# Decode lots of a paged attention in eight pieces of one matmul form each, values in one piece, no closing product

## The reference, cut to what matters

```
def fox_attend(q, c_q, segments):          # 8 heads of 64
    for k, _, c_k, mask in segments:
        s = einsum('bqhd,bkhd->bhqk', qf, k) + cq - c_k
    p = softmax(concatenate(logits, axis=-1))
    for k, v, _, _ in segments:            # past pages, then the new tokens
        out += einsum('bhqk,bkhd->bqhd', p[..., start:start + n], v)

def wkv_step(S, inp):                      # the recurrence, token by token
    sa = einsum('bhij,bhj->bhi', S, a_t)
    S = S * w_t + sa * b_t + v_t * k_t
    y = einsum('bhij,bhj->bhi', S, r_t)
```

## Time and profile before

| | us |
|---|---|
| median of 3 runs | 1510.46 |
| lowest, highest | 1509.58, 1511.0 |
| profiled execution, its time | 1510.73 |
| profiled execution, span from first to last instruction | 1509.0 |
| lots and recurrence steps, within the span | 331 to 912 |

### The profile page before, as it was taken

How to read it: one execution, slowest core, us unless ns; L and a number is a source line. 1 busy time by engine, 2 the same in 40 slices (tenths; PEclk the granted TensorE clock), 3 DMA queues, 4 the chain that set the end, 5 groups by cost and what they waited for, 6 DMA issues and landing times.

```text
span 1509.0 us, 27895 instructions
## 1 busy us (share of the span) xinstructions
PE 1402.4 (93%) x11595; PEld 953.3 (63%) x11595; DVE 438.2 (29%) x917; ACT 357.0 (24%) x713; POOL 110.0 (7%) x223
## 2 busy tenths in 40 slices
PE   5999999988799999999989779999999999999997
PEld 4755666655577777777755454477777777744442
DVE  5022355455844444444445241310000000000002
ACT  3010233245444343443433331100000000000011
POOL 6283000000000000001202010000000000000000
PEclk9999899998799999999989889999999999999998
DMA  5187011023898787878957897003111221150001
GB/s 206 57 189 205 7 57 35 1 75 110 284 312 277 229 292 247 294 255 266 272 191 261 315 314 245 1 13 100 56 56 56 89 79 56 56 195 0 0 0 63
DMA packets 123174, 219.32 MB, mean 145 GB/s; under 512 B 11451, under 2 KB 35078, under 8 KB 123046
## 3 DMA queue, kind: packets, MB, share of 16 engines
q1 hardware_dynamic: 115154, 193.64, 38.3%
q0 software_dynamic: 7824, 23.85, 5.9%
q10 hardware_dynamic: 68, 0.02, 0.0%
HBM read 203.06 MB, written 14.41 MB: 144 GB/s over the span
## 4 chain that ended last, share of the span: by engine, by line
PE 84%; DVE 5%; DMA 4%; ACT 3%; issue 2%; SPq 1%; POOL 0%; DVEq 0%; POOLq 0%; ACTq 0%
PE PS L1369 23%; PE PS L736 13%; PE PS L1388 10%; PE PS L1178 6%; PE PS L1192 4%; PE PS L1308 4%; PE PS L1237 4%; PE PS L709 2%; DMA arena<-in_cache_k 2%; DMA out_wkv_prompt<-arena 1%; PE PS L1394 1%; PE PS L992 1%; PE PS L1002 1%; PE PS L996 1%; ACT arena L1622 1%
## 5 line engine op out<-in xcount | busy, mean ns | idle before, releaser
L1369 PE MATMUL PS<-arena 128*128 128x288 f32 x1408 | 342.1, 405 | 1.2 <-DVE arena L2251 1.2
L1369 PEld LDWEIGHTS PS<-arena 128*128 128x128 f32 x1408 | 265.7, 189 | 77.4 <-DVE arena L2251 1.4
L736 PE MATMUL PS<-arena 128*128 128x301 f32 (+1 forms) x736 | 197.7, 426 | 0.0
L1622 ACT ACTIVATE arena<-PS 128x512 f32<-128x512 f32 x256 | 141.4, 596 | 192.8 <-PE PS L1178 192.4
L1178 PE MATMUL PS<-arena 128*128 128x128 f32 x1024 | 153.8, 296 | 27.1 <-DMA arena<-in_cache_k 15.1
L736 PEld LDWEIGHTS PS<-arena 128*128 128x128 f32 (+1 forms) x736 | 136.6, 189 | 54.7 <-issue 13.6
L1178 PEld LDWEIGHTS PS<-arena 128*128 128x128 f32 x1024 | 122.1, 151 | 55.8 <-issue 24.2
L1388 PE MATMUL PS<-arena 128*128 128x512 f32 x352 | 151.5, 592 | 1.5 <-DVE arena L2277 1.5
L1388 PEld LDWEIGHTS PS<-arena 128*128 128x128 f32 x352 | 66.5, 189 | 86.2 <-issue 84.3
L2277 DVE TENSOR_TENSOR arena<-PS,arena 128x576 f32<-128x576 f32 x22 | 16.7, 758 | 327.0 <-ACT arena L1686 327.0
L1686 ACT ACTIVATE arena<-PS 128x576 f32<-128x576 f32 x22 | 14.3, 651 | 329.8 <-PE PS L1369 329.8
(11 more groups left out here) (360 smaller groups left out, 1409.9 us busy)
## 6 DMA issues: line engine op xcount, KB each, us to landing
arena<-in_cache_k SPq DMA_DIRECT2D x256, 256.0 KB, 4.3
arena<-in_cache_v SPq DMA_DIRECT2D x256, 256.0 KB, 4.8
arena<-in_w_gate SPq DMA_DIRECT2D x11, 1024.0 KB
arena<-in_w_up SPq DMA_DIRECT2D x11, 1024.0 KB
arena<-in_w_in SPq DMA_DIRECT2D x5, 2048.0 KB, 11.9
forgets_after<-arena POOLq DMA_DIRECT2D x64, 128.0 KB, 8.5
arena<-forgets_after SPq DMA_DIRECT2D x32, 256.0 KB, 5.1
arena<-in_w_down SPq DMA_DIRECT2D x4, 2048.0 KB
```

The costliest lines, as they stand in the source:

```text
L736: ins = mm(PS[0:width, bank, 0:HALF], wring[:, c % 2, k, c0:c0 + width], xnT[:, k, half * HALF:(half + 1) * HALF], start=(k == 0), stop=(k ...
L1369: ins = mm(PS[:, 4 * (f % 2) + 2 * w + half, 0:HO], fring[r % FR][:, c:c + P], hT[:, k, half * HO:(half + 1) * HO], start=(k == 0), stop=( ...
L1622: av(KTs[:, (2 * i + q) % LOT], PS[:, T_USE[("k", L, i, q)] % 2, :].rearrange("p (g n) -> p g n", g=NG), ACT.Copy)\
```

## The change

- The pieces of lot L on TensorE are now: (0) keys 0; (1) scores 3 of lot L-1, and at a pair's first lot new_scores; (2) keys 1; (3) scores 0; (4) keys 2, then the turned probabilities of lot L-1; (5) scores 1; (6) keys 3, at a pair's first lot after turn_new; (7) scores 2 and all four value pages of lot L-1, at a pair's first lot also new_values, then turn_output. Scores 3 of the last lot come behind the loop.
- ScalarE: exp_lot(L-1) follows take_keys(L, 1) in piece 2 (before: it came ahead of it). VectorE: add_scores(L-1), and add_new, move to piece 1; take_probs to 4, add_sums to 5, add_output to 7.
- The closing product is gone; add_output waits for the count v_free of the last value product, and ov_ready now counts new_values alone.
- SyncE loads key pages 0 to 3 of a lot and then value pages 0 to 3 of the one before.
- A table RWKV_DUE gives one step after nearly every odd piece, and after an even one where the steps have fallen behind (20 or so in all). The last step comes after piece 239 of 256, before after 236.

```
--- before.py
+++ after.py
@@ -288,20 +288,25 @@
             T_READ.append((reader, n))
 
         for L in range(LOTS + 1):
-            for i in range(LOT + 1):
-                if i == 2 and L:
+            for i in range(LOT):
+                if i == 3 and L:
                     use_t(("p", L - 1), "pr_taken", L)
-                if i < LOT and L < LOTS:
+                if i == 3 and L % NLOT == 0 and L < LOTS:
+                    use_t(("n", L // NLOT), "prn_taken", L // NLOT + 1)
+                if L < LOTS:
                     for q in range(2):
                         use_t(("k", L, i, q), "kt_taken", 2 * LOT * L + 2 * i + q + 1)
-                if L % NLOT == 0:
-                    if i == 2 and L < LOTS:
-                        use_t(("n", L // NLOT), "prn_taken", L // NLOT + 1)
-                    if i == 3 and L:
-                        use_t(("o", L // NLOT - 1), "o_done", L // NLOT)
+            if L % NLOT == 0 and L:
+                use_t(("o", L // NLOT - 1), "o_done", L // NLOT)
+
+        RWKV_DUE = []
+        for piece in range(8 * LOTS):
+            done, aim = RWKV_DUE[-1] if piece else 0, 1 + (piece + 1) * N_RWKV / (8 * LOTS - 14)
+            RWKV_DUE.append(min(N_RWKV, done + (done < aim if piece % 2 else done < aim - 1)))
+        assert RWKV_DUE[-1] == N_RWKV
 
         def rwkv_due(piece):
-            return min(N_RWKV, 1 + piece * (N_RWKV - 1) // (8 * LOTS - 20))
+            return RWKV_DUE[piece]
 
         x2 = at(XR0, NTILE, D)
         hT = at(qT_off, KT, OUTC)
@@ -443,14 +448,10 @@
                 if not first:
                     load_bias(pr, j)
                 numbers = lot_numbers(pr, j)
-                for i in range(3):
+                for i in range(LOT):
                     key_page(pr, j, numbers, i)
                 if vj is not None:
-                    for i in range(2):
-                        value_page(vpr, vj, value_numbers, i)
-                key_page(pr, j, numbers, 3)
-                if vj is not None:
-                    for i in range(2, LOT):
+                    for i in range(LOT):
                         value_page(vpr, vj, value_numbers, i)
                 if first:
                     load_bias(pr, j)
@@ -1227,18 +1228,15 @@
                              start=True, stop=True, skip_group_check=True)
                 ins.then_inc(S["ov_ready"], 1)
 
-            def lot_values(L, half):
-                if half == 0:
-                    pe.wait_ge(S["pr_taken"], L + 1)
-                    pe.wait_ge(S["ov_taken"], L + L // NLOT + 1)
-                for i in range(2 * half, 2 * half + 2):
+            def lot_values(L):
+                pe.wait_ge(S["pr_taken"], L + 1)
+                pe.wait_ge(S["ov_taken"], L + L // NLOT + 1)
+                for i in range(LOT):
                     pe.wait_ge(v_in[i], 32 * (L + 1))
                     for r in range(4):
                         ins = mm(PS[ROWS[r], OUT, 0:QW], PTs[:, i, ROWS[r]], Vr[:, i, r // 2, QW * (r % 2):QW * (r % 2) + QW],
                                  start=(i == 0), stop=(i == LOT - 1), skip_group_check=True)
                     ins.then_inc(S["v_free"], 1)
-                if half:
-                    mm(PS[:, OUT, 511:512], ident, ones[:, 0:1], start=False, stop=True, skip_group_check=True).then_inc(S["ov_ready"], 1)
 
             def turn_output(pr):
                 pe.wait_ge(S["o_scaled"], pr + 1)
@@ -1252,33 +1250,32 @@
                     pr, j = L // NLOT, L % NLOT
                     turn_keys(L, 0)
                     yield
+                    if L:
+                        page_scores(L - 1, 3)
+                    if j == 0 and L:
+                        new_scores(pr)
+                    yield
                     turn_keys(L, 1)
+                    yield
                     page_scores(L, 0)
                     yield
+                    turn_keys(L, 2)
                     if L:
                         turn_probs(L - 1)
                     yield
-                    turn_keys(L, 2)
                     page_scores(L, 1)
                     yield
-                    if L:
-                        lot_values(L - 1, 0)
                     if j == 0:
                         turn_new(pr)
-                    yield
                     turn_keys(L, 3)
+                    yield
                     page_scores(L, 2)
-                    yield
                     if L:
-                        lot_values(L - 1, 1)
-                    yield
-                    page_scores(L, 3)
+                        lot_values(L - 1)
                     if j == 0:
+                        new_values(pr)
                         if L:
                             turn_output(pr - 1)
-                        new_values(pr)
-                    if j == NLOT - 1 and pr + 1 < NPAIR:
-                        new_scores(pr + 1)
                     yield
 
             pe.wait_ge(S["proj_taken"], len(ITEMS))
@@ -1292,6 +1289,8 @@
                     next(rest)
                     done += 1
             assert done == N_RWKV and next(rest, 1) == 1
+
+            page_scores(LOTS - 1, 3)
 
             def rows_of(i):
                 return (slice(64, P), slice(SEQ, OUTC)) if i == 0 else (slice(0, P), slice((i - 1) * P, i * P))
@@ -1320,8 +1319,7 @@
             project(0)
             turn_probs(LOTS - 1)
             project(1)
-            for half in range(2):
-                lot_values(LOTS - 1, half)
+            lot_values(LOTS - 1)
             project(2)
             turn_output(NPAIR - 1)
             project(3)
@@ -1636,18 +1634,18 @@
                     pr, j = L // NLOT, L % NLOT
                     take_keys(L, 0)
                     yield
+                    yield
+                    take_keys(L, 1)
                     if L:
                         exp_lot(L - 1)
-                    take_keys(L, 1)
+                    yield
                     yield
                     if L and j == 0:
                         exp_new(pr)
-                    yield
                     take_keys(L, 2)
                     yield
                     yield
                     take_keys(L, 3)
-                    yield
                     yield
                     yield
 
@@ -2136,12 +2134,12 @@
 
             def add_output(L):
                 q = L // NLOT % 2
-                dve.wait_ge(S["ov_ready"], L + L // NLOT + 2)
+                dve.wait_ge(S["v_free"], LOT * (L + 2))
                 dve.wait_ge(S["ov_taken"], L + L // NLOT + 1)
                 stt(Ov[:, q], Ov[:, q], Sb[:, L % 2, 0:1], PS[:, OUT, 0:QW], ALU.mult, ALU.add).then_inc(S["ov_taken"], 1)
 
             def first_output(pr):
-                dve.wait_ge(S["ov_ready"], (NLOT + 1) * pr + 1)
+                dve.wait_ge(S["ov_ready"], pr + 1)
                 v.tensor_copy(Ov[:, pr % 2], PS[:, OUT, 0:QW]).then_inc(S["ov_taken"], 1)
 
             def scale_output(pr):
@@ -2167,28 +2165,29 @@
                     pr, j = L // NLOT, L % NLOT
                     yield
                     if L:
-                        add_sums(L - 1)
+                        add_scores(L - 1)
+                    if j == 0 and L:
+                        add_new(pr)
+                    yield
+                    yield
                     yield
                     if L:
                         take_probs(L - 1)
                     yield
+                    if L:
+                        add_sums(L - 1)
                     yield
                     if j == 0:
                         take_new_probs(pr)
                     yield
-                    yield
                     if L:
                         add_output(L - 1)
-                    if j == 0 and L:
-                        scale_output(pr - 1)
-                    yield
-                    add_scores(L)
                     if j == 0:
                         if L:
+                            scale_output(pr - 1)
+                        first_output(pr)
+                        if L:
                             take_output(pr - 1)
-                        first_output(pr)
-                    if j == NLOT - 1 and pr + 1 < NPAIR:
-                        add_new(pr + 1)
                     yield
 
             dve.wait_ge(S["rn_taken"], 1)
@@ -2252,6 +2251,7 @@
                 ins.then_inc(S["xnT_ready"], 1)
 
 
+            add_scores(LOTS - 1)
             add_sums(LOTS - 1)
             take_probs(LOTS - 1)
             add_residual(0)
```

96 lines of the change are left out of this document (47 added, 49 removed).

## The result

The changed kernel takes 1539.79 us (median of 4 runs, 1530.01 to 1548.62), the kernel before 1510.47 beside it (1509.58 to 1511.0): ratio 1.0193, 95% interval 1.0131 to 1.0255. It is slower by 29 us, where the prediction had 6.5 less. The four runs of the changed kernel had mean TensorE clocks of 0.936, 0.941, 0.944 and 0.951 of full speed, with 1548.6, 1538.9, 1540.7 and 1530.0 us: by and large its time follows its clock. The profiled execution is the slowest of them (1548.6 us, span 1546.8).

What follows compares the result with a forecast made beforehand. TensorE's own stream was taken to bound 412 to 780 us, waits or bytes other stretches. Savings 13.3 + 13.5, less 11.7, 7.0 and 1.4, gave 6.7 us: 1504.0 us from 1510.73, range 1492 to 1514.

Steps and rivals of the forecast that it cites:

- the two crowded stretches: SyncE's loads around the output weights and the residual inputs: less slack but less queued behind, 0, ends 6 us either way.
- rival (e): Twelve transposes in a row take the clock to 1.2 GHz for one keys piece a lot: 27 us, 1531; chance 0.02.
- Recurrence steps: -1.4 us (ends 0 and -5): Steps whose answer is not fully covered by pieces: five more TensorE waits of 0.2 to 0.3 us each.
- Closing product, 9.6 + 0.3: Two instructions a lot removed: 0.31 us in each of 31 lots, and 0.3 us for the last lot's.
- Rival (d): Closing product nearly free, its 0.31 us going into what follows: 8 us less gain, 1512; chance 0.03.
- Probabilities behind keys 2: In piece 4 the turned probabilities wait for ScalarE's copy to free a PSUM bank: 26 lots x 0.45, -11.7 us.
- rival (a): The bank wait is the long one, ScalarE's step copies ahead each time: 7.3 us more, 1511; chance 0.15.
- The pair chain: At lots 8, 16 and 24, scores 0 wait for add_new, behind ScalarE's later exponential: 3 x 2.3, -7.0 us.
- a clock below 1.00 there: Sign in ordinary lots of the middle stretch, 412 to 780 us, that would make the prediction wrong.
- rival (b): Value burst in SyncE's queue between piece 7 and the next piece 1 starves loads: 22 us, 1526; chance 0.10.
- The sum for the middle: Lots 4 to 27, where a saving on TensorE counts: all terms together a gain of 6.7 us.

Runs made afterwards that it cites:

- run 10: Changed kernel with run 8's six filling products on 64 rows, 1527.73 us, or with a stationary operand of 64 columns, 1526.66 us.
- run 12: Kernel before with only the closing product taken out: 1504.68 us, ratio 0.9964.
- run 3: Changed kernel with the old table of recurrence steps, last step after piece 236: 1523.91 us, ratio 1.0061.
- run 7: Changed kernel with seven table entries changed, putting the recurrence steps of lot 25 one piece or more later: 1536.57 us, ratio 1.0155.
- g2: Same kernel as run 7: changed kernel with later recurrence steps in lot 25, same instructions up to lot 25; 1536.57 us.
- e2: Changed kernel with the closing product and its semaphore put back behind the four value pages: 1530.12 us, ratio 1.0132.
- e1: Changed kernel with its values in two pieces again and SyncE's loads in the old order: 1539.31 us, ratio 1.0175.
- run 11: Changed kernel with six 512-column products behind keys 0 of lot 0: on 128 rows 1536.25 us, 64 rows 1547.59, 128 rows by 32 columns 1531.09.
- run 8: Changed kernel with six unused 128-row, 512-column products around new_scores(0), two ahead and four behind: 1524.85 us, ratio 1.0079.

## Why the prediction was wrong

**The step that failed** is the price of the two crowded stretches, "0, with ends of 6 us either way", and under it the clock. The sum has no term for the clock; it appears only in rival (e), with "Only idle time is seen ahead of the half clock here: chance 0.02". That observation was wrong in the kernel before already: at 869.6 us (run 10) the clock fell behind 32-row work without any idle time. And I took the time at 1.2 GHz as a constant of the two stretches and never asked what ends it. In rows that I had, the rises at 340, 364 and 791 us stood right behind 16 transposes (335.61, 360.27 and 787.21) or in the scores after them. In lot 0 the change leaves 8 transposes in a row and puts a step of 64 or 32 rows between. What the runs showed in its place is 78 us more at 1.2 GHz, some 25 of them in the start, 7 in the middle and 48 in the end, and 12 us more idle time. The ground of (e), transposes in a row, was wrong as well: 16 transposes stand right ahead of the rise at 791.0, and 412 to 780 us with 12 in a row ran at 0.98. The Trainium skill (TensorE: Matmul & The Clock Gate, Part 4) says that transposes don't count as busy for the clock gate; the timeline of before disagrees, for transposes of float32: from 787.21 to the rise at 791.0 TensorE did nothing else.

**The size.** Measured +12.2 at the start and +24.2 at the end, in the slowest of the four executions, and not by DMA: the waits for in_cache_k and in_cache_v together were 17.9 us before (15.1 and 2.8) and are 14.8 after. Half of the added time at 1.2 GHz, 12 and 24 us, is as large.

**"Recurrence steps: -1.4 us (ends 0 and -5)".** I counted waits of TensorE behind steps only in the middle, and there it held within its ends (L993 and L1003: 3.1 us, 1.1 before). I did not count what the moved steps put ahead of the lots' own work on VectorE. At the start that is take_new_probs behind the reciprocal, 3.5 us (none before); at the end, VectorE's step work behind add_scores and add_output, so that L1109 waits 6.4 us in 3 (3.4 in 2 before) and L1119 4.3 in 2 (1.4 in 1). Behind such waits the clock was low; what it costs then depends on when it comes back.

**Closing product, 9.6 + 0.3.** Right: 0.3 a lot in run 12, 0.31 predicted. The Trainium skill's 60 cycles of overhead for an instruction (TensorEngine Tiling (Array Packing), Instruction Overhead) would have given 0.05; the run speaks for the row. Rival (d) is out.

**Waits.** Probabilities behind keys 2: 26 waits, 12.2 us, 18 of them in the middle with 6.5, at 0.36 each and one of 2.7 in lot 1; predicted 0.34 idle (0.45 of starts) 26 times. Right, and rival (a) is out. The pair chain: 3 waits, 6.8 us, predicted 3 x 2.3 (6.9; the sum has 7.0). Right as a wait, but behind those of lots 8 and 16 (ended at 504.27 and 634.34) the clock was low for 3.4 us each, which the term left out; the prediction had named a clock below 1.00 there as a sign that it was wrong. No wait for keys over 0.2 us between 412 and 780: rival (b) is out, at a DMA share of 0.81 there, as before.

**The sum for the middle.** Of 6.7 us for lots 4 to 27, 20/24 or 5.6 fall on these 20 lots. Measured 3.3; over nine profiled executions with the same middle 0.6 to 5.6, on average 3.1. With the old table (run 3) it is 5.8. So the sum had the right sign and almost twice the size, on average 2.5 us too much on 20 lots; the half clock behind the pairs' waits, 3.4 us each, costs up to 1.7 of it each time. It stood for a fifth of the time, and the other parts decided.

**What stays open.** In the end stretch, how much each new wait and the spacing of the steps contribute by themselves: run 7 mended the spacing alone without gain, and mending both was not tried. What decides whether a run of 128-row work brings the clock back: 4.3 us of it did in g2 and e2 and did not in the changed kernel and e1; keys and scores alone (3 us at 1.2 GHz) were followed by a rise at 382 us in the changed kernel and by none at 346 and 353. The changed kernel's runs spread over 18 us; its end, which took 165 to 181 us with the same instructions, is as wide, but why it varies is the same open question.

## What to carry to other kernels

A clock that fell has to be earned back, and a busy engine is not enough for it: here the rises came in 128-row work or within about 1 us behind it, and none came in 10.6 us of 64-row work. Before cutting a stream into evenly mixed pieces, look in the timeline for what stands right behind each wait of 2 us or more, and try to keep the full-row pieces together there. Look at the clock of several executions: the same instructions cost up to 7 us more or less in one lot. When steps are moved by one table on several engines, go through the queue of each engine, not of the busiest: a 0.3 us copy that falls behind a 4 us instruction holds a PSUM bank and with it TensorE. And a gain measured where the engine is full says nothing of the stretches at either end; make their sum too.

## What the runs showed that I had not expected

- TensorE can be busy without a gap and stay at 1.2 GHz: 10.6 us of 64-row products (run 11), nearly all of lot 29's 22.4 us, and the 37.0 busy of 41 us in lots 0 and 1. The same 64-row products, begun at 2.4 GHz, did not bring it down in 3.7 us (run 10), while groups on 32 rows did in the kernel before, without idle time. The Trainium skill (TensorE: Matmul & The Clock Gate, Part 1) says that activity releases the throttle; run 11 shows that activity on half of the rows did not, in 10.6 us, where the same on all rows did.
- With a stationary operand of 32 columns on 128 rows the clock came back in the fill as with one of 128 columns (run 11).
- 5.6 us of useless products in idle time made the changed kernel 15 us faster by the medians (run 8); 8 us of that are seen in the start.
- The same instructions, with nearly the same idle times, ran at 1.2 GHz for 7 and 10 us behind the wait for the first key in two executions (e2, g2) and for 48 and 58 us in two others (after, e1).
